# The hybrid mixer of a fused decoder block: attention steps inside a streamed projection, crossed PE quarters, and four scan groups that start together

## The chip, the cores and the metric

The kernel is one program on one core of a Trainium2 chip. It computes a whole two-layer stack twice over (a first block of two layers and a second block of two layers) in float32. The metric is the device time in microseconds (us) of the program. Engines are called as in the profile: PE (TensorE, matmuls), DVE (VectorE), ACT (ScalarE), POOL (GpSimd) and SP (SyncE, which here issues the DMAs of weights).

## The reference, cut to what matters

The change touches one stage alone: `hybrid_mixer` of layer 0 of the second block. Its input is 512 tokens, 256 of the main sequence and 256 of the context (four tiles of 128 tokens), normed and modulated.

```python
def hybrid_mixer(h_lat, h_ctx, ...):
    p_lat = h_lat @ w_in            # 1024 -> 3328 columns: 1792 for the recurrence, 3 x 512 for attention
    p_ctx = h_ctx @ w_in
    rc = rwkv_prepare(p_ctx[..., :RWKV_COLS], ...)   # p + (centred_shift(p) - p) * mu, norms, gates
    rl = rwkv_prepare(p_lat[..., :RWKV_COLS], ...)
    yc, sf, sb = wkv_bidir(rc, (s_zero, s_zero))     # delta-rule scans, forward and backward, 8 heads of 64
    yl, _, _ = wkv_bidir(rl, (sf, sb))
    a_lat = rwkv_output(yl, rl, r_k, ln_w, ln_b)
    o_l = diff_attn_latent(rope_2d(ql, ...), ql, rope_2d(kl, ...), kc, concatenate([vl, vc]), lam)
    out_lat = concatenate([a_lat, subln(o_l)], axis=-1) @ w_out      # and the same for the context

def wkv_scan(r, decay, k, v, kk, b, s0, reverse):
    def step(s, inp):
        sa = einsum('bhvk,bhk->bhv', s, -kk_t)
        s = s * w_t[:, :, None, :] + sa[..., None] * b_t[:, :, None, :] + v_t[..., None] * k_t[:, :, None, :]
        return s, einsum('bhvk,bhk->bhv', s, r_t)

# a = sigmoid(a0 + ad @ a_up); the decay is exp(-exp(-0.5) * sigmoid(w0 + tanh(wd) @ w_up))
# kmod = k * (1 + (a - 1) * k_a); bonus = sum(r * kmod * r_k) * v
```

## The kernel before, in words

**Products in three parts.** A float32 weight is split into a high part (ACT, L256 or L290) and a low part (DVE, L263 or L298), both of the faster type fp32r, and each product of two split operands is three matmuls (`three_products`, L312 to L314). The attention and the scans multiply plain float32; one such matmul is two PE instructions in the profile.

**The projection.** `hybrid_mixer` first runs `gemm_token_major`: seven column chunks (six of 512 columns, one of 256), each in four units of 256 rows of weights, each unit for four token tiles. Two halves of four PSUM banks take turns. ACT and DVE copy two tiles each from the banks to `rows`. Nothing else is computed beside it. The first tiles of its input come from `modulated_input`.

**Tracks.** After that, work is written as generators. Every `yield` ends a step; a loop at the end of `hybrid_mixer` (`while running`) asks each running generator for a step in turn, so that the program order on each engine is a round robin. Each generator has a chain with a semaphore `steps_done`, and a step waits for the step before it. All engines work through their instructions in program order.

- `mixed_tokens` (`pre`): for each sequence and tile 8 float32 matmuls (L2726, L2727) shift the tokens, DVE subtracts (L2735), POOL multiplies by mu (L2744); after two tiles DVE adds (L2753). Then come norms of keys, tanh and sigmoid, and the gate product (L2761 to L2839). A tile's matmuls wait for the DVE step before them, and those of the second sequence wait for L2753.
- `differential_attention`, two generators (two heads each): transposes (L2908), rotation (L2937 to L2958), then for each of four tiles and two heads a block of 11 steps: scores (L2985), maximum (L2994), exponential (L3009), combination (L3033), transposes (L3042), product with the values (L3060), scaling (L3069). Both are listed twice in the round robin.
- `scan`, four groups (direction d, half q of the heads), each with four chunks (`chunk`) of 128 tokens. A chunk has a front (L3369 to L3566: decays, gates, transposes, Gram products), five levels of a blockwise inversion of a 64 x 64 triangular matrix (L3576, ACT L3587, L3595 and L3597, DVE L3607, mask on POOL L3528), and a back (L3624 to L3748: corner, outputs, state). In a level the 64 x 64 blocks lie on the diagonal of the PE array: block b is read from rows b and written to columns b (`of_block`), so two of the four quarters of the array are in use.
- `outputs`: `attention_norms` and then `delta_rule_output` for tiles 2, 3, 1, 0, each as soon as both directions of a tile are done.

The groups of direction 0 start when `mixed_tokens` is done, and those of direction 1 when the attention is done and `STAGGER` = 25 rounds have passed. The order of tiles is 2, 3, 0, 1 in direction 0 and 3, 2, 1, 0 in direction 1. When everything is done, `feature_major` turns the results (L1291, L1302), the weights of `w_out` are loaded, and the next product begins (L312 again, at 2436.8 us of the span).

In the front of a chunk four products of 128x256 elements run on POOL (L3429, L3437, L3450, L3456) beside DVE steps of the same size (L3424, L3442, L3443, L3445). ACT takes the sigmoid at L3386 and exponentials at L3409 to L3418; when the function changes, an ACT_TABLE_LOAD precedes it.

## Time and profile before

| what | value |
|---|---|
| median of three runs | 3561.38 us (3558.02 to 3565.43) |
| profiled execution | 3568.06 us, span 3566.3 us |
| PE busy, whole span | 3255.4 us (91%) |
| DVE, ACT, POOL busy | 1893.3, 1406.6, 354.1 us |
| granted TensorE clock, mean | 0.944 |
| first matmul of the mixer's projection | 1766.17 us |
| last copy of it and first attention transposes | about 1911 us |
| first scan step (L3369) | 1990.7 us |
| last scan step (L3730) | 2415.5 us |
| first matmul of the product with `w_out` | 2436.8 us |

The span runs from the first to the last instruction of the profiled execution; about 1.8 us of its time lie outside. Busy time of PE counts the modelled length of pipelined matmuls, so that the distance from one start to the next says more than the mean length. The granted clock is 1.00 at the upper level of 2.4 GHz and 0.5 at the lower of 1.2 GHz; a value between is a mean over a stretch.

### The profile page before, as it was taken

To read this page: it belongs to the slowest core of one execution; us is meant where nothing else is said; L and a number is where in the kernel's file an instruction comes from. 1 tells how busy PE (TensorE), PEld (TensorE's weight loads), DVE (VectorE), ACT (ScalarE), POOL (GpSimd) and SP (SyncE) were. 2 spreads that over 40 slices of the span, in tenths; PEclk is the share of its full clock that TensorE was granted. 3 is DMA by queue.
4 is the path that set the end of the run, shared out by engine and by line. 5 is a ranking of instruction groups with operands and counts; after the bars stand their busy time and mean duration, and the time that the engine had idled before them with its cause. 6 is when DMAs were issued, how large, how long until landed. Compare 5 with 4: busy or idle time off the path is not lost.

```text
span 3566.3 us, 54709 instructions
## 1 busy us (share of the span) xinstructions
PE 3255.4 (91%) x22888; PEld 2800.9 (79%) x22888; DVE 1893.3 (53%) x2581; ACT 1406.6 (39%) x2039; POOL 354.1 (10%) x387
## 2 busy tenths in 40 slices
PE   8999999999999999999898689897999979896897
PEld 7877887897987788789685578786788868786795
DVE  4456645445445664544524766654333367676554
ACT  4355444435444544443521433322323244412443
POOL 2000000100100000010101243321000001033000
PEclk9999999999999999999999889898999999987999
DMA  9755656675765565575440000002232223500454
GB/s 274 221 158 171 185 152 202 197 228 181 234 206 154 153 199 151 182 227 160 146 132 12 1 8 2 2 2 95 77 96 94 78 78 88 142 1 12 142 177 135
DMA packets 449228, 459.78 MB, mean 129 GB/s; under 512 B 18288, under 2 KB 347184, under 8 KB 449008
## 3 DMA queue, kind: packets, MB, share of 16 engines
q1 hardware_dynamic: 428624, 385.08, 36.6%
q0 software_dynamic: 20384, 71.52, 6.0%
q8 instruction: 167, 2.74, 0.3%
q14 instruction: 53, 0.43, 0.0%
HBM read 455.50 MB, written 1.05 MB: 128 GB/s over the span
## 4 chain that ended last, share of the span: by engine, by line
PE 75%; DVE 14%; ACT 5%; issue 3%; DMA 2%; POOL 0%; DVEq 0%; SPq 0%; ACTq 0%; POOLq 0%
PE banks L312 20%; PE banks L313 20%; PE banks L314 20%; DVE weights_lo L298 1%; DMA raw_weights<-in_w_ffn_gu 1%; PE banks L4352 1%; PE banks L3595 1%; PE banks L3597 1%; PE banks L3576 1%; ACT weights_hi L290 1%; PE banks L1291 1%; PE banks L1902 1%; PE banks L1932 1%; DVE arena L3998 1%; DVE first_input_split L1302 1%
## 5 line engine op out<-in xcount | busy, mean ns | idle before, releaser
L298 DVE TENSOR_TENSOR weights_lo<-raw_weights,weights_hi 128x1024 fp32r<-128x1024 f32 (+2 forms) x399 | 472.9, 1186 | 505.8 <-ACT weights_hi L290 429.5
L290 ACT ACTIVATE weights_hi<-raw_weights 128x1024 fp32r<-128x1024 f32 (+2 forms) x399 | 409.6, 1028 | 610.3 <-PE banks L314 562.0
L263 DVE TENSOR_TENSOR weights_lo<-raw_weights,weights_hi 128x1024 fp32r<-128x1024 f32 x180 | 223.1, 1241 | 471.0 <-ACT weights_hi L256 281.9
L256 ACT ACTIVATE weights_hi<-raw_weights 128x1024 fp32r<-128x1024 f32 x180 | 190.6, 1060 | 515.4 <-PE banks L314 510.2
L312 PE MATMUL banks<-first_input_split,weights_hi 128*128 128x256 f32 (+1 forms) x1218 | 354.6, 291 | 13.6 <-DVE weights_lo L298 6.8
L314 PE MATMUL banks<-first_input_split,weights_lo 128*128 128x256 f32 (+1 forms) x1218 | 348.4, 286 | 0.0
L313 PE MATMUL banks<-first_input_split,weights_hi 128*128 128x256 f32 (+1 forms) x1218 | 347.1, 285 | 0.0
L298 DVE TENSOR_TENSOR third_weights_split<-raw_weights,third_weights_split 128x1024 fp32r<-128x1024 f32 (+1 forms) x173 | 207.2, 1197 | 199.9 <-ACT third_weights_split L290 156.0
L312 PE MATMUL banks<-work_split,weights_hi 128*128 128x512 f32 (+2 forms) x776 | 272.4, 351 | 18.9 <-DVEq L2459 15.0
L290 ACT ACTIVATE third_weights_split<-raw_weights 128x1024 fp32r<-128x1024 f32 (+1 forms) x173 | 178.9, 1034 | 248.8 <-PE banks L314 225.9
L313 PE MATMUL banks<-input_split,weights_hi 128*128 128x512 f32 (+2 forms) x776 | 270.7, 349 | 0.0
L314 PE MATMUL banks<-work_split,weights_lo 128*128 128x512 f32 (+2 forms) x776 | 270.4, 348 | 0.0
L312 PEld LDWEIGHTS banks<-first_input_split,weights_hi 128*128 128x128 f32 (+1 forms) x1218 | 232.7, 191 | 30.9 <-issue 20.0
L313 PEld LDWEIGHTS banks<-first_input_split,weights_hi 128*128 128x128 f32 (+1 forms) x1218 | 233.6, 192 | 0.7
L314 PEld LDWEIGHTS banks<-first_input_split,weights_lo 128*128 128x128 f32 (+1 forms) x1218 | 231.2, 190 | 0.8
L312 PE MATMUL banks<-weights_hi,first_input_split 128*128 128x512 f32 x508 | 207.3, 408 | 7.5 <-DVE first_input_split L1302 4.6
L313 PE MATMUL banks<-weights_lo,first_input_split 128*128 128x512 f32 x508 | 202.5, 399 | 0.0
L314 PE MATMUL banks<-weights_hi,first_input_split 128*128 128x512 f32 x508 | 202.4, 399 | 0.0
L312 PE MATMUL banks<-first_input_split,third_weights_split 128*128 128x256 f32 x590 | 173.2, 294 | 11.7 <-DVE third_weights_split L298 4.7
L312 PEld LDWEIGHTS banks<-work_split,weights_hi 128*128 128x128 f32 (+1 forms) x776 | 147.8, 190 | 41.0 <-issue 11.6
L312 PE MATMUL banks<-weights_hi,work_split 128*128 128x512 f32 (+1 forms) x416 | 162.8, 391 | 17.3 <-DVE work_split L266 6.0
L313 PE MATMUL banks<-first_input_split,third_weights_split 128*128 128x256 f32 x590 | 170.4, 289 | 0.0
(598 smaller groups left out, 7190.4 us busy)
## 6 DMA issues: line engine op xcount, KB each, us to landing
raw_weights<-in_w_ffn_gu SPq DMA_DIRECT2D x176, 512.0 KB, 4.9
raw_weights<-in_w_in SPq DMA_DIRECT2D x144, 512.0 KB, 3.6
raw_weights<-in_mlp_w SPq DMA_DIRECT2D x128, 512.0 KB, 3.9
arena<-in_ada_w POOLq DMA_DIRECT2D x96, 512.0 KB, 6.2
raw_weights<-in_w_ffn_down SPq DMA_DIRECT2D x80, 512.0 KB, 3.4
raw_weights<-in_w_branch SPq DMA_DIRECT2D x48, 512.0 KB, 3.6
raw_weights<-in_ssd_w_in SPq DMA_DIRECT2D x48, 512.0 KB, 3.9
raw_weights<-in_w_mkv SPq DMA_DIRECT2D x32, 512.0 KB, 4.2
```

The source lines that it names most:

```text
L256: last = s.activation(self.w_hi[:, u % 2, :], self.raw[:, u, :], ACT.Copy)
L263: last = v.tensor_tensor(self.w_lo[:, u % 2, :], self.raw[:, u, :], self.w_hi[:, u % 2, :].bitcast(F32), ALU.subtract)
L290: last = s.activation(hi, raw, ACT.Copy)
L298: last = v.tensor_tensor(lo, raw, hi.bitcast(F32), ALU.subtract)
L312: pe.matmul(out, left_hi, right_hi, start=start, stop=False)
L313: pe.matmul(out, left_hi, right_lo, start=False, stop=False)
L314: return pe.matmul(out, left_lo, right_hi, start=False, stop=stop)
L1291: last = pe.transpose(bank(q)[:, j, :], src, c.ident[:, :])
L1302: last = v.tensor_tensor(place(lo, q), bank(q), place(hi, q).bitcast(F32), ALU.subtract)
L1902: last = pe.matmul(c.ps[strip:strip + STRIP, bank, columns], c.conditions[:, 2 * k:2 * k + STRIP], slot[:, j, half * SEQ:(half + 1) * SEQ] ...
L1932: last = pe.matmul(c.ps[:, 7, at:at + 2], mod_rows[:, i, j % 2 * P:(j % 2 + 1) * P], pick[:, j // 2, :], start=True, stop=True)
L3576: last = pe.matmul(g.of_block(b, h, 256), block(g.level, b, h), block(g.inv_t, b, h), start=True, stop=True)
```

## The change

1. **Streamed projection.** `HybridInput` replaces the two calls of `gemm_token_major`. It yields after each unit and tile (112 pieces of six matmuls), uses banks 0 to 3 alone, splits units two ahead, and takes all copies with ACT. The attention's columns come first: k, q, v, then the 256 narrow columns, then k, r, v of the recurrence.
2. **Attention beside it.** From the end of the second chunk on, `beside` takes one and two steps by turns of each attention generator after each piece; their PE instructions stand between the pieces. The blocks wait for the third chunk. Buffers of the attention and of `mixed_tokens` move (`c.raw`, `c.spare` and `c.x_t` to `c.z` and `c.work`). In `mixed_tokens` only the place of the wait for the attention moves.
3. **Front of a chunk.** sigmoid(x) becomes 0.5 * tanh(x / 2) + 0.5 (ACT tanh and one more DVE step). Four POOL products and the first mask go to DVE. One bonus product stays on POOL, in level 2, with its sum on DVE in level 4.
4. **Crossed quarters.** The first product of a level goes from rows b to columns 1 - b, and the second step uses all four quarters in turn (rows 1 - b to columns b in the first bank, rows 1 - b to columns 1 - b in the second). The first transposition needs 16 matmuls for each group where it needed 8, and one copy of 128x512 where it was 128x256.
5. **Start.** All four scan groups and `outputs` start in one round, once `mixed_tokens` and the attention are done. `STAGGER` is gone.

```diff
-STAGGER = 25
 class Mixing:
-        self.delta = cols(w, 0, ROWS, Q_AT)
+        self.deltas = [cols(x_t, 0, NT, Q_AT), cols(w, 7680, NT, Q_AT)]
 def differential_attention(c, m, n, ch, attended, values):
-    qr_t, qp_t, qc_t, kr_t = (c.raw[:, i, :].rearrange("p (h t) -> p h t", t=SEQ) for i in range(4))
-    kc_t = cols(x_t, 3072, 4, SEQ)
+    qr_t, qp_t, qc_t, kr_t, kc_t = (cols(w, i * 1024, 4, SEQ) for i in range(5))
...
-    while len(attended) < 2:
+    while len(attended) < 2 or not values():
         yield
+class HybridInput:
+    def __init__(self, c, a, x):
+        self.chunks = [(q + RW, RW), (q, RW), (q + 2 * RW, RW), (low, SEQ), (r + RW, RW), (r, RW), (r + 2 * RW, RW)]
+        self.units = [unit for at, width in self.chunks for unit in token_units(a["hy_w_in_2"][0], at, width)]
...
+    def take(self, chunk, t):
+        @c.block.scalar
+        def _(s):
+            if t < ROWS - 1:
+                s.wait_ge(c.projected, chunk * (ROWS - 1) + t + 1)
+            else:
+                s.wait_ge(c.multiplied, self.first + (chunk + 1) * UNITS + 2)
+            s.activation(self.rows[:, t, at:at + width], c.ps[:, t, 0:width],
+                         ACT.Copy).then_inc(c.projection_taken, 1)
+    def run(self):
+        for chunk, (_, width) in enumerate(self.chunks):
+            for u in range(UNITS):
+                n = chunk * UNITS + u
+                self.split_ahead(n + 2)
+                for t in range(ROWS):
+                    @c.block.tensor
+                    def _(pe):
+                        if t == 0:
+                            pe.wait_ge(c.lo_made, first + n + 1 + UNITS)
+                        if u == 0 and chunk > 0:
+                            pe.wait_ge(c.projection_taken, (chunk - 1) * ROWS + t + 1)
+                        for j in range(per_unit):
+                            last = c.three_products(pe, c.ps[:, t, 0:width], x_hi[:, k, tokens], x_lo[:, k, tokens],
+                                                    hi[:, j, :], lo[:, j, :], k == 0, k == KD - 1)
+                    if u == UNITS - 1:
+                        self.take(chunk, t)
+                    yield
 def hybrid_mixer(c, a, out, projection):
-    c.gemm_token_major(range(ROWS), 6, column_chunks(a["hy_w_in_2"][0], 0), BANK,
-                       *token_copies(c, rows, range(ROWS)), more=True, tiles_made=c.tiles_made)
+    def beside():
+        while projection.taken < 2 * ROWS:
+            yield
+        for n in itertools.count():
+            for s in attention * (1 + n % 2):
+                if s in attention and next(s, True):
+                    attention.remove(s)
+            yield
+    both = beside()
+    for _ in projection.run():
+        next(both)
     # in chunk()
-            s.activation(g.sigs, g.sigs, ACT.Sigmoid).then_inc(ch.steps_done, 1)
+            s.activation(g.sigs, g.sigs, ACT.Tanh, scale=0.5).then_inc(ch.steps_done, 1)
+            v.tensor_scalar(g.sigs, g.sigs, 0.5, 0.5, ALU.mult, ALU.add).then_inc(ch.steps_done, 1)
...
-            p.tensor_tensor(g.kks, g.kks, kk_g, ALU.mult).then_inc(g.pooled, 1)
-            p.tensor_tensor(g.rho, r_g, g.e_in, ALU.mult).then_inc(ch.steps_done, 1)
+            v.tensor_tensor(g.kks, g.kks, kk_g, ALU.mult).then_inc(ch.steps_done, 1)
+            v.tensor_tensor(g.rho, r_g, g.e_in, ALU.mult)
...
-                last = pe.matmul(g.of_block(b, h, P), block(g.inv, b, h), blockwise[b * HD:(b + 1) * HD, 8, :],
+                one = blockwise[b * HD:(b + 1) * HD, 8, :]
+                pe.matmul(block(g.sums(0), b, h), block(g.inv, b, h), one, start=True, stop=True)
+                last = pe.matmul(block(g.sums(1), 1 - b, h), one, block(g.inv, b, h), start=True, stop=True)
...
-                    last = pe.matmul(g.of_block(b, h, 256), block(g.level, b, h), block(g.inv_t, b, h), start=True,
+                    last = pe.matmul(g.of_block(1 - b, h, 256), block(g.level, b, h), block(g.inv_t, b, h),
...
-                    pe.matmul(g.of_block(b, h, P), block(g.inv, b, h), block(g.half, b, h), start=True, stop=True)
-                for b, h in blocks:
-                    last = pe.matmul(g.of_block(b, h, 0), block(g.half, b, h), block(g.inv, b, h), start=True,
+                    inv, half = block(g.inv, 1 - b, h), block(g.half, 1 - b, h)
+                    pe.matmul(block(g.sums(0), b, h), inv, half, start=True, stop=True)
+                    last = pe.matmul(block(g.sums(1), 1 - b, h), half, inv, start=True, stop=True)
     # the loop at the end of hybrid_mixer()
-                if s is pre:
-                    running += [scan(g, chain_ends([mixing])) for g in groups[0:2]]
...
-        if late and after is not None and ticks >= after + STAGGER:
-            running += [scan(g, chain_ends([mixing] + attend)) for g in groups[2:4]]
+        if not begun and not running:
+            begun = True
+            running = [scan(g, chain_ends([mixing] + attend)) for g in (groups[0], groups[2], groups[1], groups[3])]
+            running.append(outputs())
```

## Rows read from the trace of the kernel before

**Rows 1.** Busy time by stretch: projection, mixing, scans, three phases of the last chunk.

```profile
core 0: us, PE busy (x) PEld busy (x) DVE busy (x) ACT busy (x) POOL busy (x), PEclk, DMA share, GB/s
1766.17:1910.40 144.23, 142.77 (x672) 119.57 (x672) 44.97 (x49) 37.75 (x45) 11.74 (x22) 1.00 0.36 105
1910.40:1990.70 80.30, 48.35 (x186) 29.12 (x184) 54.48 (x59) 24.32 (x45) 16.67 (x4) 0.82 0.00 1
2092.40:2361.30 268.90, 239.33 (x4738) 221.98 (x4731) 176.37 (x350) 90.52 (x210) 102.73 (x122) 0.92 0.02 4
2348.50:2371.40 22.90, 19.82 (x240) 17.58 (x238) 19.59 (x41) 9.69 (x20) 9.05 (x11) 1.00 0.01 1
2371.40:2392.80 21.40, 18.05 (x497) 17.17 (x497) 12.26 (x21) 4.69 (x13) 7.55 (x9) 0.92 0.01 3
2392.80:2415.60 22.80, 21.52 (x128) 19.99 (x128) 2.49 (x7) 2.96 (x8) 0.00 (x0) 0.55 0.00 1
```

**Rows 2.** Timeline of PE, mixing and attention: start, length, what, idle before.

```profile
1911.95 1.09 PE L2908 MATMUL banks<-identity,arena 128*128 128x128 f32 x8 [1.40 <-DVE arena L922]
1912.88 0.92 PE L2726 MATMUL banks<-arena 128*128 128x448 f32 x2
...
1918.14 0.92 PE L2727 MATMUL banks<-arena 128*128 128x448 f32 x2
...
1939.45 1.86 PE L2726 MATMUL banks<-arena 128*128 128x448 f32 x2 [9.36 <-DVE arena L2753]
...
1975.79 2.05 PE L3060 MATMUL banks<-arena 128*128 128x128 f32 x16
1977.68 3.60 PE L2808 MATMUL banks<-arena 128*128 128x512 f32 x8
...
1981.75 0.60 PE L2985 MATMUL banks<-arena,raw_weights 64*128 64x256 f32 x4
1982.18 0.60 PE L2985 MATMUL banks<-raw_weights 64*128 64x256 f32 x4
...
1988.81 1.97 PE L3042 MATMUL banks<-identity,spare 128*128 128x128 f32 x8 [5.61 <-DVE spare L3033]
```

**Rows 3.** Groups of the mixing, 1910 to 2420 us: busy, mean ns, idle before.

```profile
L2744 POOL TENSOR_TENSOR arena<-arena 128x1792 f32<-128x1792 f32 x4 | 16.7, 4168 | 164.8 <-DVE arena L2735 164.8
L2735 DVE TENSOR_TENSOR arena<-banks,arena 128x1792 f32<-128x1792 f32 x4 | 8.1, 2025 | 15.4 <-PE banks L2727 15.4
L2753 DVE TENSOR_TENSOR arena<-arena 128x3584 f32<-128x3584 f32 x2 | 7.8, 3884 | 0.0
```

**Rows 4.** Busy time by stretch: end of the mixing, then the last tile's output.

```profile
1969.90:1987.50 17.60, 10.82 (x56) 7.86 (x56) 12.52 (x19) 11.33 (x18) 0.00 (x0) 0.79 0.00 1
2415.60:2426.50 10.90, 4.28 (x24) 4.05 (x24) 9.88 (x15) 3.88 (x8) 3.76 (x2) 0.66 0.00 0
```

**Rows 5.** Groups of a chunk's front, 1910 to 2420 us.

```profile
L3445 DVE TENSOR_TENSOR arena<-arena 128x256 f32<-128x256 f32 x16 | 14.5, 906 | 1.9 <-POOL arena L3429 1.9
L3409 ACT ACT_TABLE_LOAD x8 | 10.3, 1283 | 0.1
```

**Rows 6.** Timeline of DVE in a front, POOL idle from 2007.3 on.

```profile
2007.42 0.41 DVE L3442 TENSOR_TENSOR arena<-arena 128x256 f32<-128x256 f32 x1
2007.76 0.41 DVE L3443 TENSOR_TENSOR arena<-arena 128x256 f32<-128x256 f32 x1
```

**Rows 7.** Timeline of PE: column halves (L3707), diagonal quarters (L3597), four quarters (L3495).

```profile
2155.39 0.69 PE L3707 MATMUL banks<-arena 128*64 128x64 f32 x16
...
2219.06 0.63 PE L3597 MATMUL banks<-arena 64*64 64x64 f32 x16
2219.53 0.28 PE L3595 MATMUL banks<-arena,spare_lo 64*64 64x64 f32 x4
...
2363.30 0.68 PE L3495 MATMUL banks<-arena 64*64 64x64 f32 x24 [0.25 <-DVE arena L3480]
2363.92 0.38 PE L3486 MATMUL banks<-arena 64*128 64x128 f32 x2
```

More of the change, by code:

```diff
@@ L3468, in _ @@
             last.then_inc(ch.steps_done, 1)
-        ch.steps += 1
+        @ch.block.vector
+        def _(v):
+            v.wait_ge(ch.steps_done, ch.steps)
+            v.tensor_tensor(g.part, g.kmod, r_k[:, g.columns], ALU.mult).then_inc(ch.steps_done, 1)
+        ch.steps += 2
         yield
@@ L3529, in masked, with _ @@
             g.pools += 1
-        masked(0)
+        @ch.block.vector
+        def _(v):
+            v.wait_ge(ch.steps_done, ch.steps)
+            v.tensor_tensor(g.level, g.lower, over_heads(blockwise[:, 0, :]), ALU.mult).then_inc(g.pooled, 1)
+        g.pools += 1
+        @ch.block.vector
+        def _(v):
+            pooled(v)
+            v.tensor_tensor(g.inv, over_heads(blockwise[:, 8, :]), g.level, ALU.subtract).then_inc(ch.steps_done, 1)
         yield
@@ L3640, in _ @@
             for h in range(half_heads):
-                last = pe.matmul(g.of_block(early, h, P), block(g.inv, early, h), block(g.half, early, h), start=True,
+                last = pe.matmul(g.of_block(early, h, P), block(g.inv, late, h), block(g.half, late, h), start=True,
                                  stop=True)
@@ L3772, in scan @@
             yield from chunk(g, tile, n == 0)
-    attend, tiles = c.attend, c.rows_chains
-    attended, in_rounds = [], {}
     mixing, pre = c.chains[0], mixed_tokens(c, m, c.chains[0], attended)
-    attention = [differential_attention(c, m, n, attend[n], attended) for n in range(2)]
     def outputs():
@@ L3797, in hybrid_mixer @@
     running = attention + attention + [pre]
-    after, ticks, late = None, 0, False
-    while running:
+    begun = False
+    while running or not begun:
         for s in list(running):
```

187 lines of the change are left out of this document (119 added, 68 removed).

## The prediction

> **What bounds the kernel now.** I read the page first (PE is busy nearly everywhere), then the busy time by stretch, because the change touches one stage only. From 1766.2 us, the first matmul of the mixer's projection, to 2436.8, the first one behind the mixer, there are 670.6 us; all else stays as it is. The stage has four parts with different limits [rows 1]. The projection (144.2 us) is PE without a gap, at clock 1.00, while DVE is busy 45 us. The mixing with the first attention blocks (80.3 us) is a chain across PE, DVE and POOL: none is busy more than 54 us, and the clock is 0.82. The scans last from 1990.7 to 2415.5 us (424.8). In their middle three chunks of four groups take 268.9 us, 89.6 each, with PE busy 239 and DVE 176. The last chunk, in which one pair of groups is alone, shows the phases: a front of 22.9 us that DVE fills (19.6), levels of 21.4 us that PE nearly fills even for two groups (18.1 at clock 0.92), and a back of 22.8 us that is PE alone at clock 0.55. The tail is one tile's output and its turning, 21.2 us. The profiled execution took 3568.06 us, 6.7 above the median; differences are worked out on it and taken off the median.
>
> **Projection with the attention, 194 us (before: 144.2).** The same products remain. Their 112 pieces are 104 in units of full width (a chunk of 256 columns counts half), so one lasts 144.2 / 104 = 1.39 us. In program order the attention's instructions stand between the pieces, so their PE time adds. Scores: 4 instructions in 0.43 us (1981.75 to 1982.18), 96 of them: 10.3 us. Values: 16 in 1.89 us (1975.79 to 1977.68), 96: 11.3. Transposes: 8 in 0.93 (1911.95 to 1912.88), 88: 10.2 [rows 2]. Sum 32 us. The stalls: from the scores of a block to its transposes the chain took 1988.81 - 1981.75 = 7.1 us from its second four instructions on [rows 2], some 7.6 in all. After the change there are seven steps at 1.5 a piece between them, some 4.7 pieces or 6.5 us, and the scores of both generators (1.8 us): enough for full pieces. In the narrow chunk a piece is half as long, 2 to 3 blocks fall into it, and each lacks about 3 us. ACT and DVE also split a unit of weights every 5.5 us (about 1.1 and 1.2 us: 37.8 and 45 us busy over 28 units and the copies [rows 1]), and with one spare buffer DVE's share waits for ACT behind the attention's exponentials: 1 to 3 us a full-width block. I take 18 us, bounds 4 and 36. 88 block steps need 59 pieces, and 64 follow the third chunk: the attention ends inside. ACT's copies move nothing: four banks come free one by one, each has three pieces (4.2 us) before its next use.
>
> **Mixing alone, 68 us.** Per tile: 16 PE instructions from 1912.88 to 1918.9 (6.0 us) [rows 2], DVE 2.0, two hops of 0.2: 8.3. Per sequence two tiles, then POOL 4.2 and DVE 3.9 [rows 3]: 25 us, twice 50. After the 9.4 us in which PE has nothing, its first instructions ran at half pace (1.86 us in place of 0.92 [rows 2]): 3 us more. The steps from L2761 on took 17.6 us with attention steps between [rows 4]; without them 15. Nothing hides this part now: before, 57 us of attention steps shared it. Bounds 62 (no clock loss, 12 at the end) and 75 (as with the attention). So the scans begin at 1766.2 + 194 + 68 = 2028 us, 37 us later than before, but with nothing else to do.
>
> **A chunk of four groups, 87 us (before: 89.6).** All four are in the same phase, so each phase takes what its fullest engine needs for four.
> - Front. A DVE step of 256 columns beside POOL takes 0.91 us [rows 5], without POOL it follows the next in 0.34 [rows 6]. A group has 15 such steps (five more than before, of which four came from POOL, and the scale-and-shift at 0.45) and four of 512 columns out of banks, by interpolation between 0.34 and 2.0 for 1792 [rows 3] 0.62 each: 7.7 us a group, 31 for four. The start (PE) and the end (PE, ACT) add 3: 34 us, bounds 31 and 42. The two table loads a pair of groups (1.28 us each [rows 5]) go, and were in that chain: in the mixing, where an exponential came before, tanh had none ahead of it.
> - Levels. Diagonal quarters: 16 instructions in 0.47 us, 29 ns each. Four quarters (L3495): 24 in 0.62 to the next line, within the group (0.68 - 0.25) / 23 = 19 ns [rows 7]. The first product keeps 0.47, the second has 32 instructions, 0.93 before and 0.60 to 0.83 now; I take 0.68. A level of four groups is 4 x 1.15 = 4.6 us of PE; ACT (1.5), DVE (2.5) and POOL (2.9) fit under it. Five levels 23, and 3 for the last one's DVE steps: 26. PE needed 5.6 a level before.
> - Back. For a pair 21.5 us busy at clock 0.55 [rows 1], 11.8 at full clock; four groups 23.7, and the first hops: 25.
> - Sum 85, and 2 for the clock, which was 0.92 over the scans too [rows 1].
>
> Here two rules of the skill speak against the sum. The row has four quarters at 19 to 26 ns an instruction. The Trainium skill (TensorE: Matmul & The Clock Gate, § Part 1) has a start-to-start floor of about 25 ns; the second product would be 0.80 us and a chunk 2.4 us longer, 9.6 in all. The row's inner 19 ns do not agree with that floor.
>
> **Whole scans, 355 us.** 4 x 87 = 348; minus 6 (no state products in the first chunk, fewer in the last); plus 13 for the attention's norms and two tiles' outputs, DVE work of 7 and 2 x 9 us that falls half into DVE's fronts. **Tail, 31 us (before: 21.2).** Tiles 1 and 0 now both end with the last chunk, and `outputs` makes them one after the other: one more output, about 10 us [rows 4]. Before, tile 1's lay beside the last chunk of direction 1.
>
> **Sum.** 194 + 68 + 355 + 31 = 648 against 670.6: 22.6 us less. 3561.4 - 22.6 = 3539.
>
> **Rivals.**
> - *The front starves PE (slower, 0.25).* Staggered, one pair's DVE front lay beside the other's PE levels; now PE waits out 34 us of every chunk but for some 15 us of short work. For it: DVE fills the front [rows 1]. If the clock then comes back only inside the levels, as it did after the 9.4 us gap, each chunk loses 3 to 4 us there, and with a front of 40 it is 96 us: 3561.4 - 22.6 + 36 = 3575. It decides from 92.6 us a chunk on. Against it: fronts of a pair kept clock 1.00.
> - *Crossing gives nothing (same, 0.13).* Two products in a row now read the same rows. L3707, two column halves over all rows, has (0.69 - 0.23) / 15 = 31 ns, no better than the diagonal [rows 7]; at that pace the second product is 0.98 us, a level 5.8, a chunk 6 us longer: 24 us, 3563. Against it: L3495 uses the same four quarters, though in another order, with rows by turns. The Trainium skill (TensorE: Matmul & The Clock Gate, § Part 3, The mechanism) says that weight loads overlap matmuls only between different row groups, which is this rival; the quick L3707, all in one row group, agrees with it at most in part.
> - *The attention holds up the projection (same, 0.10).* If each of the eight blocks costs 4 us in stalls, that part is 212 us and the total 3557.
> - *Everything overlaps (0.10).* 80 us a chunk (front 31, levels 24, back 24) and 184 us for the first part: 3501.
> - *Forecast as summed, 3524 to 3554: 0.42.*
>
> Changes under 0.2% (7 us) can't be told from none. Faster: 0.42 and 0.10 and small mixtures, 0.57. Same: 0.18. Slower: 0.25. The range reaches from the fast case to the slow one, 3502 to 3577; the forecast's own range is 3524 to 3554.
>
> **What would show it.** (1) PE between the first and last product of the projection: about 194 us, clock near 1.00, attention lines between pieces. (2) Mixing alone of 68 us, POOL and DVE alternating. (3) Chunks about 87 us apart, by the adds after L3369's products; POOL nearly idle in fronts, 256-column DVE steps 0.34 us apart, no table load inside a chunk. (4) The level's second product 0.6 to 0.8 us a group. (5) About 31 us from the last scan step to the next product. It is wrong if a chunk is over 93 us, through fronts over 40 us or a clock under 0.85, or if the projection part passes 215 us.

## The result, and the profile after

The changed kernel took 3607.88 us (median of three, 3573.77 to 3610.12), the kernel before 3561.38 (3558.02 to 3565.43): ratio 1.010, 95% interval 1.0064 to 1.0137. It is 1.0% slower, where 3539 was forecast, and the median lies outside the range of 3502 to 3577 (one of the three runs, 3573.77, lies inside). Repeated in six runs (e5 below) it took 3608.37, ratio 1.0139 (1.0113 to 1.0164). Ratios leave out runs more than 1.5% above the fastest of their own kernel (one of e2's four, three of e3's ten, four of e17's six); medians hold all.

The profiled execution after is one of 3607.88 us (span 3606.1), that of before one of 3568.06 (3566.3). Busy time by stretch, in the columns of [rows 1]; the stretches are the projection with the attention, the mixing alone, the scans, the tail, and then front, levels and back of the second chunk, and the back of the last:

```profile
1760.20:1956.50 196.30, 180.46 (x950) 146.47 (x951) 81.40 (x154) 76.99 (x155) 11.77 (x22) 1.00 0.26 78
1956.50:2028.10 71.60, 37.44 (x84) 17.58 (x82) 24.15 (x13) 9.74 (x12) 15.85 (x4) 0.75 0.00 0
2028.10:2447.20 419.10, 348.15 (x6560) 320.07 (x6560) 233.91 (x541) 108.23 (x269) 73.50 (x98) 0.76 0.01 3
2447.20:2476.80 29.60, 12.30 (x41) 8.31 (x41) 23.49 (x39) 9.66 (x16) 4.51 (x3) 0.60 0.29 103
...
2134.20:2167.00 32.80, 25.93 (x356) 22.51 (x354) 32.27 (x80) 9.96 (x26) 2.96 (x4) 0.76 0.01 2
2167.00:2195.60 28.60, 21.67 (x997) 20.30 (x994) 14.14 (x28) 8.77 (x22) 13.89 (x20) 1.00 0.02 4
2195.60:2243.00 47.40, 46.24 (x331) 43.31 (x321) 5.32 (x18) 6.10 (x16) 0.00 (x0) 0.52 0.00 1
2409.40:2447.20 37.80, 37.76 (x197) 35.57 (x194) 1.26 (x3) 4.03 (x11) 0.00 (x0) 0.50 0.00 0
```

The last two rows matter most. PE is busy 46.24 of 47.40 us and 37.76 of 37.80, DVE, ACT and POOL do next to nothing, and the granted clock is 0.52 and 0.50. In the 28.6 us before, where PE is busy only 21.67, it is 1.00.

| part | forecast | before | after |
|---|---|---|---|
| projection (with attention after) | 194 | 144.2 | 196.3 |
| mixing (with attention before) | 68 | 80.3 | 71.6 |
| scans | 355 | 424.8 | 419.1 |
| tail | 31 | 21.2 | 29.6 |
| sum | 648 | 670.6 | 716.6 |

The stage became 46.0 us longer; the projection began 6.0 us earlier (1760.2 against 1766.2), so the span grew by 39.8. Of 68.6 us between forecast and measurement 64.1 are in the scans. Over those, 197.2 us passed at the lower clock (before: 96.7): 126.5 in three of the four backs, the rest mostly in fronts.

The back of one chunk kept the clock. These are the four backs from the first output product (L3799) to the next chunk's first step, the last one to its own last step; then the first three of e3 (the changed kernel with the crossing undone, below), which kept it:

```profile
2100.40:2132.90 32.50, 32.50 (x195) 31.44 (x194) 1.86 (x6) 4.74 (x11) 0.00 (x0) 0.50 0.00 1
2201.10:2244.60 43.50, 41.70 (x258) 39.15 (x258) 3.49 (x12) 3.45 (x9) 0.00 (x0) 0.50 0.00 1
2319.10:2342.80 23.70, 22.79 (x257) 21.30 (x256) 2.72 (x10) 5.11 (x11) 0.00 (x0) 1.00 0.01 2
2409.70:2447.20 37.50, 37.46 (x193) 35.39 (x192) 1.26 (x3) 3.75 (x10) 0.00 (x0) 0.50 0.00 0
...
2110.00:2127.50 17.50, 17.50 (x195) 16.86 (x192) 1.86 (x6) 5.30 (x12) 0.00 (x0) 1.00 0.01 2
2195.80:2220.50 24.70, 22.89 (x260) 21.39 (x258) 3.53 (x12) 4.00 (x11) 0.00 (x0) 1.00 0.00 1
2297.50:2321.30 23.80, 22.89 (x260) 21.37 (x258) 2.76 (x10) 5.28 (x12) 0.00 (x0) 1.00 0.00 1
```

The same number of matmuls takes 32.5 us or 17.5, and 43.5 or 23.7. The end of a group's chunk on DVE shows the same pace: first two ends of the first chunk, then two of the third.

```profile
2119.01 0.43 DVE L3859 COPY arena<-banks 128x256 f32<-128x256 f32 x1 [21.09 <-PE banks L3847]
2123.67 0.42 DVE L3859 COPY arena<-banks 128x256 f32<-128x256 f32 x1 [4.04 <-PE banks L3847]
...
2332.53 0.42 DVE L3859 COPY arena<-banks 128x256 f32<-128x256 f32 x1 [13.80 <-PE banks L3847]
2335.66 0.42 DVE L3859 COPY arena<-banks 128x256 f32<-128x256 f32 x1 [2.52 <-PE banks L3847]
```

They are 4.66 us apart in the first and 3.13 in the third, though a back of the first chunk has fewer products (it has no state yet). In the second chunk, whose products are those of the third, they are 5.7 us apart. The same in PE's timeline, at the border from the last step of the levels (L3773) to the back (L3799), first chunk:

```profile
2099.74 0.74 PE L3773 MATMUL banks<-arena,raw_weights 64*64 64x64 f32 x5
2100.40 3.89 PE L3799 MATMUL banks<-arena 128*128 128x64 f32 x17
```

Seventeen instructions of 64 columns in 3.89 us, 0.23 each, and neither row has idle time before it.

The fronts are close to the forecast: DVE's steps of 256 columns follow each other in 0.34 us, as in [rows 6].

```profile
2143.99 0.41 DVE L3557 TENSOR_TENSOR arena<-arena 128x256 f32<-128x256 f32 x1
2144.33 0.42 DVE L3558 TENSOR_TENSOR arena<-arena 128x256 f32<-128x256 f32 x1
```

The levels hold two surprises. The crossed second product (L3729, L3730) is much quicker than forecast. Where nothing interrupts it, the 128 instructions of the four groups start between 2287.79 and 2289.71 us, 15.1 ns apart, 0.48 us a group. The first and last rows of that stretch:

```profile
2287.79 0.28 PE L3730 MATMUL banks<-arena 64*64 64x64 f32 x2
...
2289.71 0.23 PE L3729 MATMUL banks<-arena,raw_weights 64*64 64x64 f32 x2
```

But PE then stands still in the middle of a group, where the program has no wait. In level 3's first product it stops after 27 of the 32 instructions of the first two groups:

```profile
2177.34 0.92 PE L3705 MATMUL banks<-arena 64*64 64x64 f32 x25
2179.68 0.34 PE L3705 MATMUL banks<-arena 64*64 64x64 f32 x5 [1.42 <-issue]
```

Over the scans these stops of the levels add up to 21.2 us in 22 places ("issue": the profile shows nothing that PE waited for). Their sum, count and longest, then the instruction queue's packets and MB from 2167 to 2196 us:

```profile
PE banks L3730 <- issue: 8.1, 8, 1.5
PE banks L3705 <- issue: 6.9, 7, 1.5
PE banks L3729 <- issue: 6.2, 7, 1.8
...
q8 instruction: 8, 0.13, 1.9%
```

In the levels of the second chunk, four of these stops come 129 or 130 matmuls after the one before, and in each of the six longest ones PE goes on 1.2 to 1.5 us after such a packet of 16 KB has landed. That reads as PE using up its instructions faster than they arrive. It is a reading of the times; no run tests it. The same sum is 20.0 us in e5 (the changed kernel again), 0.2 in e3 (crossing undone), 7.0 in e10 and nothing in e1 and e6 (starts apart).

### The profile page after: what moved, and what is told of

Same layout as the page of the kernel before. It is cut to its first block and busy times, and to the rows that moved or that the text cites. A ratio compares the mean times of both kernels' runs of the same rounds, so it can differ in the third digit from the quotient of the medians.

```text
span 3606.1 us, 55058 instructions
## 1 busy us (share of the span) xinstructions
PE 3252.1 (90%) x23144; PEld 2790.4 (77%) x23144; DVE 1875.8 (52%) x2647; ACT 1398.4 (39%) x2038; POOL 294.5 (8%) x323
## 5 line engine op out<-in xcount | busy, mean ns | idle before, releaser
L299 DVE TENSOR_TENSOR weights_lo<-raw_weights,weights_hi 128x1024 fp32r<-128x1024 f32 (+2 forms) x427 | 504.6, 1183 | 567.9 <-ACT weights_hi L291 493.1
L291 ACT ACTIVATE weights_hi<-raw_weights 128x1024 fp32r<-128x1024 f32 (+2 forms) x427 | 437.5, 1026 | 657.8 <-PE banks L315 603.6
L264 DVE TENSOR_TENSOR weights_lo<-raw_weights,weights_hi 128x1024 fp32r<-128x1024 f32 x152 | 188.9, 1244 | 374.1 <-ACT weights_hi L257 185.9
L257 ACT ACTIVATE weights_hi<-raw_weights 128x1024 fp32r<-128x1024 f32 x152 | 161.0, 1060 | 414.4 <-PE banks L315 409.0
L313 PEld LDWEIGHTS banks<-first_input_split,weights_hi 128*128 128x128 f32 (+1 forms) x1218 | 231.3, 190 | 34.3 <-issue 20.2
```

Of the source, the lines that this page charges most:

```text
L257: last = s.activation(self.w_hi[:, u % 2, :], self.raw[:, u, :], ACT.Copy)
L264: last = v.tensor_tensor(self.w_lo[:, u % 2, :], self.raw[:, u, :], self.w_hi[:, u % 2, :].bitcast(F32), ALU.subtract)
L291: last = s.activation(hi, raw, ACT.Copy)
L299: last = v.tensor_tensor(lo, raw, hi.bitcast(F32), ALU.subtract)
L313: pe.matmul(out, left_hi, right_hi, start=start, stop=False)
```

## The experiments

"Scans", "low" (time of the scans at the lower clock) and "tail" are those of each kernel's profiled execution; the medians are of all runs. The profiled execution need not be a typical one: it is the fastest of e2, e4, e7, e8 and e10, and the slowest of e12, e15, e16, e17 and e18. e4 and e13 give wrong results, as said below.

| kernel | median us (runs) | ratio, 95% | scans | low | tail |
|---|---|---|---|---|---|
| e5 changed, again | 3608.37 (6) | 1.0139, 1.0113 to 1.0164 | 417.1 | 195.2 | 29.7 |
| e2 before, joint start | 3618.05 (4) | 1.0195, 1.0133 to 1.0257 | 373.4 | 75.1 | 29.3 |
| e1 pairs 24 rounds apart | 3565.66 (10) | 1.0014, 0.9998 to 1.0030 | 376.8 | 112.7 | 29.7 |
| e6 directions 24 apart | 3565.15 (12) | 1.0016, 1.0001 to 1.0032 | 379.9 | 106.8 | 21.8 |
| e10 directions 12 apart | 3557.46 (12) | 0.9997, 0.9985 to 1.0009 | 369.5 | 103.3 | 22.2 |
| e16 directions 16 apart | 3568.79 (12) | 1.0021, 1.0007 to 1.0036 | 392.5 | 136.5 | 21.8 |
| e11 directions 36 apart | 3559.62 (12) | 1.0002, 0.9992 to 1.0012 | 375.5 | 87.4 | 21.8 |
| e3 crossing undone | 3577.39 (10) | 1.0012, 0.9991 to 1.0033 | 389.5 | 123.3 | 29.4 |
| e9 crossing undone, 24 apart | 3568.91 (12) | 1.0026, 1.0015 to 1.0038 | 385.1 | 51.2 | 21.8 |
| e4 wide filler in the backs | 3625.07 (4) | 1.0187, 1.0163 to 1.0211 | 421.8 | 75.1 | 29.6 |
| e13 narrow filler in the backs | 3760.91 (4) | no interval | 521.1 | 162.8 | 29.8 |
| e7 filler in the fronts | 3641.42 (4) | 1.0247, 1.0212 to 1.0282 | 428.1 | 152.7 | 29.6 |
| e15 wide filler ahead of backs | 3584.80 (5) | 1.0063, 1.0041 to 1.0085 | 400.1 | 87.7 | 29.5 |
| e17 narrow filler ahead | 3673.62 (6) | 1.0199, 1.0152 to 1.0247 | 486.2 | 221.9 | 29.6 |
| e18 one wide ahead | 3604.38 (6) | 1.0124, 1.0092 to 1.0156 | 430.1 | 208.2 | 29.5 |
| e14 12 apart, two wide ahead | 3569.65 (12) | 1.0024, 1.0006 to 1.0043 | 389.3 | 109.4 | 22.0 |
| e8 24 apart, bonus late | 3575.74 (9) | 1.0052, 1.0030 to 1.0073 | 370.0 | 81.8 | 21.9 |
| e12 as e9, bonus late | 3571.70 (8) | 1.0033, 1.0020 to 1.0045 | 387.2 | 62.9 | 21.8 |

### The start: e2, e1, e6

e2 is the kernel before with the changed one's start and nothing else; e5 is the changed kernel unchanged. e1 and e6 are the changed kernel with two groups begun later: in e1 one of each direction, in e6 both of direction 1.

```diff
-    running = [scan(g, ...) for g in (groups[0], groups[2], groups[1], groups[3])]
+    def delayed(rounds, track):
+        for _ in range(rounds):
+            yield
+        yield from track
+    running = [delayed(w, scan(groups[n], ...)) for n, w in [(0, 0), (1, 0), (2, 24), (3, 24)]]   # e6
```

> The kernel before, with only the start of the scans changed: all four groups and the outputs begin in one round when the mixing and the attention are done. The attention ends at about 2068 us, so the scans begin some 77 us later than before and end after four chunks. Clock theory: the backs in a row lose the clock here too, chunks of 105 to 118 us, scans of 430 to 460 us from 2068 on, median 3640 to 3700 us. If the start together is harmless and the loss lies in the other parts, chunks stay at 90 us: 3561 + 77 - (425 - 360) + 8 = about 3580.

> The changed kernel, with groups 1 and 3 started 24 rounds (about half a chunk) after groups 0 and 2. Clock theory (the backs of four groups in a row bring the granted clock to its lower level while PE never idles, 2197.8 to 2249.0 us of the changed kernel's trace, some 23 us a chunk): the backs of one pair now lie beside levels and fronts of the other, the mean clock of the scans rises from about 0.75 to over 0.9, a chunk falls from 98-112 us to at most 88, and the median is 3520 to 3550 us. Starved-front theory (PE idle in the DVE-bound fronts brings it down): the same direction, since fronts are covered too, so this run does not tell the two apart; the filled backs do. In-order theory (what is slow is that the round robin makes groups wait for one another, whatever the clock): a chunk stays at or above 98 us and the median above 3590.

> The changed kernel once more, with more executions, as the base for the others. Clock theory: its executions spread over some 40 us (3570 to 3610), and each one's time goes with its mean granted clock, about 3 us for each 0.001. In-order theory: the spread has nothing to do with the clock.

> The changed kernel with groups 2 and 3 (the second direction) started 24 rounds after groups 0 and 1. Theory: staggered backs keep the clock (spread under 20 us), and tile 1's output falls beside the last chunk as it did before, so that the tail is 21 us in place of 30: 3552 to 3560 us, against 3565.7 of the pairs by half. If tile 1's output costs as much inside the scans, the time is as with the pairs by half, 3562 to 3570.

Undone in the changed kernel, the joint start gives back 42.7 us (e1) and 43.2 (e6), less than the clock theory of e1 forecast (3520 to 3550). e5's six runs lie within 15 us, where 40 were expected. e2 lies between its two expectations, and it does two things at once: the scans wait for the attention (they begin at 2053.5 us, before at 1990.7), and all groups are in step. Its scans, forecast at 430 us or more if the backs lose the clock, took 373.4 in the profiled execution, the fastest of four (3587.75). All four of its backs kept the clock:

```profile
2125.40:2142.90 17.50, 17.50 (x195) 16.85 (x192) 1.86 (x6) 5.29 (x12) 0.00 (x0) 1.00 0.00 1
2212.00:2236.70 24.70, 22.89 (x260) 21.39 (x258) 3.54 (x12) 5.26 (x12) 0.00 (x0) 1.00 0.01 1
2313.80:2337.50 23.70, 22.79 (x257) 21.30 (x256) 2.73 (x10) 5.20 (x12) 0.00 (x0) 1.00 0.01 1
2406.50:2426.90 20.40, 20.40 (x194) 19.16 (x192) 1.26 (x3) 3.98 (x11) 0.00 (x0) 1.00 0.01 2
```

Against the execution before, it ends the scans 11.8 us later and has 8 us more of tail, about its whole loss. Its other three runs (3617.65, 3618.46 and 3659.66, mean clock 0.932, 0.934 and 0.920 against 0.942) are slower still. So a joint start lets backs lose the clock; it does not make them. e1 and e6 split on the tail, 29.7 and 21.8 us: directions that end together cost 7.9 of the 10 us that the forecast charged, and e6's scans are 3.1 us longer, so at the median nothing is left of it.

### The crossing: e3, e9

```diff
-    inv, half = block(g.inv, 1 - b, h), block(g.half, 1 - b, h)
-    pe.matmul(block(g.sums(0), b, h), inv, half, start=True, stop=True)
-    last = pe.matmul(block(g.sums(1), 1 - b, h), half, inv, start=True, stop=True)
+    pe.matmul(g.of_block(b, h, P), block(g.inv, b, h), block(g.half, b, h), start=True, stop=True)
+for b, h in blocks:
+    last = pe.matmul(g.of_block(b, h, 0), block(g.half, b, h), block(g.inv, b, h), start=True, stop=True)
...   # the first product, the first transposition, their copies and the corner go back as well
```

> The changed kernel with the products of the levels back on the diagonal quarters. Theory that crossing pays: the second product takes 29 instead of 23 ns an instruction, 0.93 instead of 0.75 us a group; over 5 levels, 4 groups and 4 chunks some 14 us more, less 3 for the shorter first transposition: 3615 to 3625 us, if the clock falls as often. Theory that crossing is worth nothing or costs the clock: no more than 3605 us.

> The changed kernel with the crossing undone and the groups of direction 1 begun 24 rounds after those of direction 0. Theory A (joint backs lose the clock, and the crossing adds to it): without the crossing the clock is steadier, mean clock 0.944 to 0.952; each level is up to 1 us longer on PE per four groups, which the other direction's work covers; 3545 to 3560 us, under the crossed version with the same start (3565). Theory B (the crossing matters only where PE is the limit of a level, and with staggered groups PE is the limit nearly everywhere): the diagonal form costs 16 levels' worth of some 0.3 us a group, about 15 to 20 us, 3578 to 3585, at the same clock as the crossed version (0.938 to 0.946).

That the crossing pays fell: with a joint start the kernel without it is 31 us faster at the median, though its ten runs spread from 3555.83 (mean clock 0.949) to 3625.40 (0.927). Its profiled execution (3588.12) lost the clock in the last back alone. So undoing the crossing gives back almost as much as undoing the joint start, and it is the two together that cost. From the first product of the levels to the back, the crossed form takes 33.4, 33.5, 33.5 and 32.5 us, the diagonal one 33.5, 33.6, 35.4 and 34.3: 3.9 us in four chunks is all that the crossing brought there (6.8 in e5), with the 21.2 us of stops shown above.

With the directions apart, e9 lies between its two expectations, and the forms differ by 3.8 us in favour of the crossed one (3568.91 and 3565.15). Scans of e9, then of e6, in the columns of [rows 1]:

```profile
2026.20:2411.30 385.10, 337.56 (x6304) 307.04 (x6304) 249.20 (x555) 107.16 (x272) 78.79 (x98) 0.93 0.01 4
```
```profile
2031.30:2411.20 379.90, 325.15 (x6560) 292.76 (x6560) 246.49 (x555) 110.55 (x272) 77.36 (x98) 0.86 0.01 4
```

The crossed form has 12.4 us less PE busy time, at a clock of 0.86, where the diagonal one ran at 0.93; over their twelve runs each, the mean clock is 0.938 to 0.946 and 0.947 to 0.956. So a part of what the crossing saves there seems to be given back as clock; no run separates the two.

### Where the clock is lost: fillers e7, e4, e13, e15, e17, e18

Added matmuls write to a part of a bank that the back does not read. e7: four of 128x256 in each front, for the theory that the front starves PE. e4: two, two and four of 128x256 ahead of the three steps of each back; their start flag resets an accumulation in their bank, so a part of y of the odd heads is lost. e13: the same columns in 32 pieces of 64, with the same loss. e15: four of 128x256 ahead of the first step only, after which nothing is lost. e17: the same columns there in 16 pieces of 64. e18: one of 128x256 there.

```diff
+        def filled(pe, times):
+            for _ in range(times):
+                pe.matmul(g.bank(1, 256, 256), c.ident[:, :], c.par[:, 0:256], start=True, stop=True)   # e13, e17: 64
...
+            filled(pe, 4)             # e15; e17: 16 of 64 columns; e18: 1; e4: 2, and 2 and 4 further down
             for h in range(half_heads):
                 last = pe.matmul(g.bank(h % 2, h // 2 * HD, HD), g.g1_t[:, h, :], head(v_g, h), start=h < 2,
```

> The changed kernel with four matmuls of 128x256 float32 in the third step of every front (where PE has little to do) and none in the backs. Starved-front theory: with PE fed in the fronts the clock stays up in the backs too, backs of 25 us, median 3560 to 3590 us in spite of up to 20 us of added work. Clock theory in the narrow form (the backs' own matmuls lose it): the fronts may keep the clock, but it falls in the backs as often as before, and the median is 3600 to 3630.

> The changed kernel with eight matmuls of 128x256 float32 (0.43 us each at the upper clock) added to the back of every group and chunk, two, two and four in its three product steps, written to a part of a bank that nothing reads: 3.4 us a group, 13.7 us a chunk, 55 us in all of added PE work. Clock theory, in the form that narrow matmuls of 64 columns are what the clock falls on: it stays at its upper level in the backs, which take 25 + 14 = 39 us instead of 48, and the median falls to 3570 to 3600 us in spite of the added work. Starved-front theory: the clock falls as before, the added matmuls run at half pace and cost over 55 us: 3660 or more.

> The changed kernel with 32 added matmuls of 64 columns in every back, as many columns in all as the 8 wide ones of the filled kernel had and at the same three places; as there, their start flag resets accumulations in their bank, so a part of y of the odd heads is lost. Theory A (the form of the work costs the clock: matmuls of 64 columns lose it though PE is never idle): the backs stay at the lower clock, mean clock 0.915 to 0.930, 3660 to 3720. Theory B (any PE work added there keeps the clock, because the back is then longer or further from the front): the backs at the upper clock, mean clock 0.945 to 0.955, about 3625 as with the wide ones.

> The changed kernel (joint start) with 4 matmuls of 256 columns ahead of the first output product of every back and none inside it: 6.9 us a chunk of four groups at full clock. Theory A (wide matmuls among the narrow ones keep the clock; in the round robin the four groups' backs lie over each other, so these count as among them): clock 0.943 to 0.952, 3590 to 3610. Theory B (they must lie inside the back): clock falls behind them, 0.928 to 0.936, 3630 to 3645.

> The changed kernel (joint start) with 16 matmuls of 64 columns ahead of the first output product of every back, as many columns as the 4 wide ones had and at the same place. Theory A (width keeps the clock): with narrow ones it falls as without, mean clock 0.920 to 0.935, 3640 to 3690. Theory B (any PE work at that place keeps it): 0.943 to 0.950, 3585 to 3600.

> The changed kernel (joint start) with 1 matmul of 256 columns ahead of the first output product of every back, 16 over the scans, 6.8 us of PE at full clock. Theory A (the clock hangs on how much wide work stands in the back): one does little, clock 0.931 to 0.937, 3600 to 3615. Theory B (a short burst at the change from levels to back is enough): clock 0.943 to 0.950, 3565 to 3580.

The starved front finds no support: e7 was 33 us slower than the changed kernel, above both expectations, and in its fastest execution two of its backs still had their ends 5.7 us apart (the other two kept the clock). In e4's fastest execution all four backs ran at 1.00 but for their first 4 us in the first chunk (low 75.1 us in place of 197.2), yet 128 matmuls cost more than the clock gave: 3625, between the two expectations. e15 shows that the lost clock is what costs: half as many wide matmuls ahead of the back make the kernel 23.6 us *faster* than the changed one (3584.80 against 3608.37; all five runs of e15 lie below the six of e5, though one of the changed kernel's first three, 3573.77, lies below them), though PE has 28.5 us more to do (128 instructions at 0.2225 us). All four backs of the profiled execution end at the quick pace (2.54, 3.13, 3.13 and 2.52 us). Its back of the first chunk:

```profile
2108.45 1.95 PE L3486 MATMUL banks<-arena,identity 128*128 128x256 f32 x8
2110.23 1.00 PE L3804 MATMUL banks<-arena 128*128 128x64 f32 x8
2111.07 1.95 PE L3486 MATMUL banks<-arena,identity 128*128 128x256 f32 x8
2112.85 1.00 PE L3804 MATMUL banks<-arena 128*128 128x64 f32 x8
```

A wide instruction takes 0.22 us (2108.45 to 2110.23 for eight), one of the back's 0.105 (2110.23 to 2111.07). e17, the same columns at the same place in narrow pieces:

```profile
2111.60 3.19 PE L3486 MATMUL banks<-arena,identity 128*128 128x64 f32 x14
2114.59 1.91 PE L3804 MATMUL banks<-arena 128*128 128x64 f32 x8
2116.30 4.05 PE L3486 MATMUL banks<-arena,identity 128*128 128x64 f32 x18
```

Here one of the back's takes 0.21 us, twice as long, and the stretches of its first two backs and of the third show the clock:

```profile
2104.50:2168.00 63.50, 63.28 (x362) 62.11 (x364) 2.42 (x9) 6.35 (x15) 0.00 (x0) 0.50 0.00 1
2234.20:2306.50 72.30, 72.00 (x424) 69.34 (x424) 2.97 (x12) 5.09 (x14) 0.00 (x0) 0.50 0.00 1
2370.00:2420.00 50.00, 46.67 (x756) 44.34 (x745) 11.18 (x31) 9.58 (x23) 0.48 (x1) 1.00 0.01 2
```

So a busy PE was not enough: 72.00 of 72.30 us busy at 0.50. A back of narrow matmuls alone may lose the clock and stay at the lower one to its end. It may also keep it, as the third and fourth here (this is the slowest of six runs; another took 3611.12 at a mean clock of 0.948), and three of four in e13, whose first back held 0.50 with PE busy in all of it:

```profile
2105.00:2120.00 15.00, 15.00 (x75) 14.88 (x73) 0.00 (x0) 1.71 (x5) 0.00 (x0) 0.50 0.00 0
...
2270.00:2312.00 42.00, 41.05 (x416) 39.97 (x416) 2.64 (x9) 2.29 (x6) 0.00 (x0) 1.00 0.01 1
```

e13 bears out neither expectation for that reason: two runs at 3711 and 3715 us (mean clock 0.938), two at 3806 and 3809 (0.911 and 0.909). One wide matmul (e18) changed nothing that can be measured: 3604, from 3589 to 3631. The times of e17 and e15 can't be compared as they stand, since the narrow pieces cost more by themselves: 512 instructions at 0.105 us are 54 us even at the upper clock. Their mean clocks can: 0.928 to 0.936 in five of e17's six runs, 0.945 to 0.950 in all five of e15. That points to the form of the work. Narrow pieces also load the weights four times as often for the same columns, and last longer; width, loads and length were not told apart.

### Distance and fillers together: e10, e16, e11, e14

The edit of e6 with 12, 16 and 36 rounds; e14 is e10 with two wide matmuls ahead of each back.

> The changed kernel, groups of direction 1 begun 12 rounds after those of direction 0 (24 before). Theory A (what counts is that the backs of the two directions do not stand together): 12 rounds are about a third of a chunk, so a back lies beside the other direction's levels; as good as 24 rounds at the clock, with a start and an end alone that are some 10 us shorter: 3553 to 3563, mean clock 0.940 to 0.946. Theory B (a back wants the other direction's front or a full half chunk of distance): backs overlap again in part, clock 0.933 to 0.938, 3575 to 3590.

> The changed kernel, groups of direction 1 begun 16 rounds later; 12 rounds gave 3557, 24 gave 3565, 36 gave 3560. Theory A (the distance matters little once the backs are apart): 3555 to 3566, clock 0.940 to 0.946. Theory B (12 is a narrow optimum): 3562 to 3575, clock under 0.941.

> The changed kernel, groups of direction 1 begun 36 rounds after those of direction 0. Theory A: the same clock as with 24 (0.940 to 0.946), but a longer stretch at the start and at the end with one direction alone: 3570 to 3580. Theory B: with 36 rounds the backs of one direction meet the fronts of the other, PE is starved least, clock over 0.946 and 3555 to 3565.

> The changed kernel, groups of direction 1 begun 12 rounds later, and 2 matmuls of 256 columns ahead of the first output product of every back, 32 of them over the scans, some 14 us of PE at full clock if nothing hides them. Theory A (wide matmuls keep the clock): mean clock 0.948 to 0.956, the gain and the price about even: 3550 to 3560. Theory B (two are too few, or the clock falls only after them): clock as without (0.939 to 0.948), 3566 to 3576.

12 and 36 rounds equal the kernel before (0.9997 and 1.0002, both intervals hold 1), 16 and 24 are 0.2% slower. That is no smooth curve, and 0.2% is little, so the runs decide little: e10 lies in the range of its theory A, e11 in that of its theory B, and e16's time is B's while its clock (0.939 to 0.947) is nearer A's. That a distance's worth hangs on where the backs fall is a guess. In e14 the mean clock was that of e10 (0.939 to 0.948 in both) and the filler was paid nearly in full, 12 us, as its second expectation had it. e10's second and third back of direction 1 lie beside the other direction's front (DVE 17.07 us busy of 27, where the backs after had 5.32 of 47.4), at 0.75 and 0.80:

```profile
2183.00:2210.00 27.00, 25.29 (x300) 23.20 (x298) 17.07 (x45) 7.54 (x20) 0.00 (x0) 0.75 0.01 2
2278.00:2313.00 35.00, 33.29 (x406) 30.45 (x406) 19.51 (x53) 9.50 (x23) 0.00 (x0) 0.80 0.01 1
```

### The bonus product: e8, e12

```diff
-            if n == 2:
+            if n == LEVELS - 2:
                 bonus_products()
-            if n == 4:
-                bonus_sums()
...   # in the corner step
+        bonus_sums()
```

> As the version staggered by direction, with the one bonus product that POOL still makes moved from level 2 to level 5, and its sum to the corner step. Theory: in level 2 POOL's product stands before other groups' masks, which the next level waits for, some 2 us a chunk; moved to level 5, where POOL has no mask, it is free: 3 to 8 us less than the version staggered by direction. Rival: with two groups in a phase POOL is not full, and nothing changes.

> The changed kernel with the crossing undone, the groups of direction 1 begun 24 rounds later, and the bonus product moved from level 2 to level 5 with its sum in the corner step. Theory A (the mask of level 3 waits about 2 us a chunk behind the bonus product, and with two directions apart other work does not cover it): 3 to 8 us less than the same kernel without the move. Theory B (with the directions apart the other direction covers the wait): the same within 3 us, or some us more as with the crossed version, where the move gave 3576 against 3565.

The gain of 3 to 8 us did not come: e8 is 10.6 us slower than e6, and e12 2.8 slower than e9 at the median, which its theory B had. The wait that both edits aim at, a level's first product behind the bonus product on POOL, is not in the changed kernel's trace: the 1.42 us shown above lie in the middle of a group. The fastest run of all changed versions (3545.14, mean clock 0.950) is one of e8, and so is one of 3585.78 (0.936). Why e8 is slower stays open, and one profile at 3545 says nothing of the median.

## Why the prediction was wrong

The step that failed is "Back. For a pair 21.5 us busy at clock 0.55 [rows 1], 11.8 at full clock; four groups 23.7, and the first hops: 25", and with it "2 for the clock". The row's low clock was taken for a matter of the one place where a pair is alone, and was left out of the other backs. The joint start puts the backs of all four groups in a row with nothing else between their matmuls, and such a back may run at the lower clock. Before, the middle of the scans ran at 0.92 [rows 1]. Measured: 47.4 us for the second chunk's phase, corner step included. At the upper clock the forecast of 25 was good: 23.7 us in the third chunk. Against backs that kept the clock, the other three lost 15.0 us (32.5 and e3's 17.5), 19.8 (43.5 and 23.7) and 17.1 (37.5 and e2's 20.4), together 52 of the 64.1 us by which the scans missed. In e5, 42.6 us in the third chunk stand against 24.6 in the second. e15 shows that the cause is the clock. The other 12 us lie in the fronts and levels; that they add up to just this is not shown.

The joint start alone does not explain it: e2 and e3, both in step but with the diagonal form, kept the clock in four and three backs of their profiled executions. Both profiled executions of the changed kernel, crossed and in step, lost it in three.

By the steps:

- Projection with the attention: 194 forecast, 196.3 measured, clock 1.00. Right, with the stalls at 20 where 18 were taken.
- Mixing alone: 68 and 71.6. Right; the clock was 0.75.
- Front: 34 and 32.8. Right, DVE busy 32.27 of it. The rival "the front starves PE" had the direction right by luck: it put its loss into the levels, which ran at 1.00, and the work that e7 put into the fronts brought no gain.
- Levels: 26 and 28.6, near by two errors that cancel. The second product took 0.48 us a group (0.68 taken, bounds 0.60 and 0.83), worth 16 us less over the 80 groups and levels; the 21.2 us of stops were not in the sum. The Trainium skill (TensorE: Matmul & The Clock Gate, § Part 1) gives a floor of about 25 ns from start to start; the 15.1 ns here lie well below it, and its 0.80 us a group were further off than 0.68.
- Back: above. The Trainium skill (same page, § HAM oscillation — how this bites in real kernels) sums up the rule as having no long idle gaps on PE. The rows here show that this is not enough: 72.00 of 72.30 us busy, and 0.50.
- Tail: 31 and 29.6. Right; e6 against e1 shows 8 us of it as the price of directions that end together.
- The rival "crossing gives nothing" was nearly right on what the crossing brings and wrong in its reason. The second product did become faster, 15.1 ns an instruction against 29; with the joint start the levels got only 3.9 us shorter in four chunks all the same, with PE stopped for 21.2 us of them.
- "The attention holds up the projection" (212 us) did not come about.
- Of the signs that it would be wrong, two appeared: chunks over 93 us (104.9, 109.8, 99.1 and 105.3, from end to end), and a clock under 0.85 (0.76 over the scans).

The range was too narrow for one reason: the clock entered as 2 us a chunk with no bound of its own. With [rows 1] as the bound from the other side (four groups' backs at 0.55: 43 us in place of 25) a case 72 us above the forecast, at 3611, would have stood in it. That it lies near the measured 3608 is partly luck: one back of four kept the clock.

**What stays open.** Why one back of a kernel keeps the clock and the next, of the same instructions, loses it, in other chunks in other runs. And why the crossed form loses it more often than the diagonal one: e3 against e5 and e9 against e6 show that it does, no run shows by what. Whether the stops in the levels are a lack of instructions, and whether they have a part in the loss of the clock behind them, no run tests.

**What there is to win.** Of the 16 versions of the changed kernel the best, e10, equals the kernel before (3557.46, ratio 0.9997, 0.9985 to 1.0009) and is 51 us faster than the changed kernel. Its profiled execution (3549.73, its fastest) has 659.7 us in the stage against 670.6. No version beats the kernel before by more than can be told from nothing.

## What to carry to other kernels

- A row with PE fully busy at a clock of 0.55 is a warning, not a factor. Ask what stood beside that work elsewhere, and whether the change puts more of the same side by side: groups in step join their narrow phases, and that can nearly double them (23.7 and 43.5 us for the same back).
- Give the clock a term with bounds of its own. Within one kernel time moved by 1 to 3.5 us for each 0.001 of mean clock (e10: 3549.73 at 0.946 to 3569.27 at 0.939), so repeat a kernel until its spread of clocks is known before a gain of 10 us is believed.
- Where groups can be staggered, the distance is to be tried in both directions; it was worth up to 51 us here.
- A quicker product is worth what the phase gets shorter. The second product was halved, and the levels got 1 to 2 us a chunk shorter: look where PE then stands still.

## What the runs showed of the hardware

- The granted clock stayed at 0.50 for 72 us of e17 with PE busy in 72.00 of 72.30 us, nearly all of it matmuls of 64 columns with 128x128 weights. The levels, in quarters of the array with 64 columns, ran at 1.00 with PE busy 21.67 of 28.60.
- Adding work can save time: 64 matmuls of 128x256 that nobody reads made the changed kernel 23.6 us faster (e15 against e5).
- The same instructions ran at either clock from one chunk to the next: backs of e17 at 0.50, 0.50 and 1.00. The second chunk's back took 43.5 us in one execution of the changed kernel and 24.6 in another.
- Four quarters of the array by turns take a 64-column float32 instruction every 15.1 ns (128 of them in 1.92 us), the diagonal every 29 [rows 7].
- At that pace PE stopped again and again, often after 129 or 130 matmuls, for up to 1.8 us, with a 16 KB packet on the instruction queue landing 1.2 to 1.6 us before it went on in the longer stops; 21.2 us over the scans, and 0.2 where the diagonal form ran (e3).
